# Routed experts: a selection made pair by pair, gates on the outcome, a scatter in two rounded terms, three chunks outside the ring

## The chip, the cores and the metric

The kernel runs on one core of a Trainium2 chip. The metric is the device time of one execution in microseconds (us). Before the change it is 2018.83 us, the median of 3 runs (2018.33 to 2025.63). PE is TensorE (matrix products), DVE VectorE, ACT ScalarE, POOL GpSimd, and SP the engine that issues most transfers.

## What is computed

A network of three blocks over 256 tokens of 1024 channels, all in float32: a first block of two layers (modulated norms, feed-forwards, a pooling mixer, latent attention), then a hybrid mixer, then the part that the change touches, a mixture of 32 experts in 4 groups, each token going to the best group and to 2 experts in it:

```python
def hier_moe(h, w_rg, b_rg, w_re, b_re, w_eg, w_eu, w_ed):     # h: 256 tokens x 1024
    lg = xt @ w_rg + b_rg;  grp = argmax(lg);  p_grp = softmax(lg)[grp]
    le = (xt @ w_re + b_re)[group grp]                          # 8 logits
    top_p, top_i = lax.top_k(jax.nn.softmax(le, axis=-1), 2)
    gate = top_p / jnp.sum(top_p, axis=-1, keepdims=True) * p_grp
    expert = grp * EXPERTS_PER_GROUP + top_i
    ...
    def expert_block(args):                                     # EXPERT_FF = 512
        xb, e = args
        return (jax.nn.silu(xb @ w_eg[e]) * (xb @ w_eu[e])) @ w_ed[e]
    y = yb[dest] * gate_s
    return jax.ops.segment_sum(y, tok_s, num_segments=n_tok)    # added to x
```

## The kernel before

All weights are packed on the host into one stream of chunks, 128 partitions x 3072 floats (1536 KB) each, in the order in which they are used. There are 304 of them. SP loads them into a ring of six slots (`ring`): chunk n is issued once the counter `chunk_used` shows that chunk n - 6 has been read (lines 212 to 216). The experts' stage uses the last 128 chunks, 8 for each of 16 pairs of experts. What is fixed by hand: each engine has its own program with its own order, and semaphores join them.

Before the stage come a norm (`pre_norm(7)`), in which ACT squares X and takes a root, and `router()`: PE computes the 36 logits and turns H into token-major HTOK, which ACT copies out of PSUM (line 1685); DVE makes the two choices of each token, their gates (block 24) and the position of each token in its expert's list (POS), and the longest list. If that is at most CAP = 64, `sparse()` runs, as with these inputs.

In `sparse()` DVE first builds SEL, for all 32 experts a matrix of 256 tokens x 64 places that holds 1 where the token has that place (line 1942, two operations of 2048 columns), and SELG, the same times the gate (line 1948). PE transposes SELG (line 1198) and ACT copies it out as SELGT (line 1694). For each pair p of experts PE then does:

- gather: XE = HTOK x SEL, 16 products into psG, which DVE copies out (line 1959)
- gate_up: 32 halves of 128 x 512 weights against XE, into the two banks of psS; ACT takes silu of the gate (line 1697), DVE multiplies with the other (line 1953)
- turn: four transposes of the hidden rows (line 1148), copied out by ACT as HT (line 1700)
- down: 16 halves against HT, into psG; DVE copies the outcome to YS (lines 1965 and 1967)
- scatter: YS x SELGT summed over all pairs in the four banks of psA, 8 products in float32

A half is a sixth of a chunk, so gate_up reads 5 1/3 chunks and down 2 2/3. The order within a step is gate_up(p), scatter(p - 1), turn(p), gather(p + 1), down(p). A float32 product shows as two records on PE, a product of the rounded type (`parts`, float32r) and a transpose as one. In the end DVE adds the four banks of psA to X (`add_acc`, line 2407), and SP writes X out in one transfer (line 219). Outside the stage all `mm` calls share line 370, so rows are told apart by their tiles.

Of the kernel before, what the change touches and what calls it, by code (L numbers as in the profile page):

```python
# [18 lines left out]
P = 128  # L19
# [6 lines left out]
RING = 6  # L26
EPS = 1e-6
# [18 lines left out]
          ("moe", E * FE)]  # L46
# [30 lines left out]
def build(nc, stream, cols_d, ident_d, x_d, masks_d, out_d):  # L77
    ctx = ExitStack()
    with ctx:
# [120 lines left out]
        def _(sp):  # L200
# [156 lines left out]
        SEL, SELG, SELGT = blk(4, 4), blk(8, 4), blk(12, 4)  # L357
        HTOK, XE, YS = tiles(16, 2, D), tiles(18, 1, P), blk(20)
# [8 lines left out]
        def _(pe):  # L367
# [735 lines left out]

            def sparse():

                c0 = BASE["moe"]  # L1110

                def gather(r, p):

                    if p == 0 and isinstance(r, int):
                        pe.wait_ge(sem("sp_sel"), 1)

                        pe.wait_ge(sem("sp_gt"), NP // 2)
                    for b in range(2):
                        for k in range(4 * b, 4 * b + 4):
                            for t in range(TT):  # L1120
                                off = t * E * CAP + p * P
                                src = SEL[:, off:off + P] if isinstance(r, int) else \
                                    SEL[:, bass.ds(r * (3 * P) + off, P)]
                                last = mm(psG[:, b, (k % 4) * P:(k % 4 + 1) * P], HTOK[:, t, k * P:(k + 1) * P],
                                          src, start=(k % 4 == 0 and t == 0), stop=(t == 1))
                        last.then_inc(sem("sp_ga"), 1)

                def gate_up(r, p):

                    pe.wait_ge(sem("sp_xe"), r * 6 + 2 * (p + 1))  # L1130
                    c = c0 + 8 * p
                    for u in range(2):
                        for k in range(KT):
                            for e in range(2):
                                g = (u * KT + k) * 2 + e
                                if g % 6 == 0:
                                    arrived(pe, c + g // 6, r * 24)
                                last = mm(psS[64 * e:64 * e + 64, u, :], XE[:, k, e * CAP:(e + 1) * CAP],
                                          half(c, g), start=(k == 0), stop=(k == KT - 1))
                                if g % 6 == 5:  # L1140
                                    last.then_inc(chunk_used, 1)
                    last.then_inc(sem("sp_gu"), 1)

                def turn(r, p):

                    pe.wait_ge(sem("sp_act"), r * 3 + (p + 1))
# [4 lines left out]
                def down(r, p):  # L1151

                    pe.wait_ge(sem("sp_htout"), r * 3 + (p + 1))
                    c = c0 + 8 * p
                    for h in range(2):
                        if p < NP - 1 or not isinstance(r, int):

                            pe.wait_ge(sem("sp_xe"), r * 6 + (2 * (p + 1) + h + 1))
                        for f in range(FE):
                            for e in range(2):  # L1160
                                g = 2 * 2 * KT + (h * FE + f) * 2 + e
                                if g % 6 == 0:
                                    arrived(pe, c + g // 6, r * 24)
                                last = mm(psG[64 * e:64 * e + 64, h, :], HT[:, f, e * CAP:(e + 1) * CAP],
                                          half(c, g), start=(f == 0), stop=(f == FE - 1))
                                if g % 6 == 5:
                                    last.then_inc(chunk_used, 1)
                        if h == 0:
                            last.then_inc(sem("sp_dn"), 1)

                def scatter(r, p, final=False):

                    pe.wait_ge(sem("sp_ys"), r * 6 + 2 * (p + 1))
                    for m in range(KT):
                        src = SELGT[:, p * S:(p + 1) * S] if isinstance(r, int) else \
                            SELGT[:, bass.ds(r * (3 * S) + p * S, S)]
                        last = mm(psA[:, m // 2, (m % 2) * S:(m % 2 + 1) * S], YS[:, m * P:(m + 1) * P], src,
                                  start=(isinstance(r, int) and p == 0 and m % 2 == 0), stop=final)
                    return last

                def step(r, p):
# [4 lines left out]
                    if not isinstance(r, int) or p < NP - 1:  # L1186
                        gather(r, p + 1)
                    down(r, p)


                pe.wait_ge(sem("sp_selg"), 1)
                pe.wait_ge(sem("htok_out"), 1)
                for p in range(NP):
                    b = p // 2
                    if p % 2 == 0 and b >= 2:
                        pe.wait_ge(sem("sp_gt"), b - 1)
                    for t in range(TT):
                        last = nc.tensor.transpose(psG[:, b % 2, ((p % 2) * 2 + t) * P:((p % 2) * 2 + t + 1) * P],  # L1198
                                                   SELG[:, t * E * CAP + p * P:t * E * CAP + (p + 1) * P], ident)
                    if p % 2 == 1:  # L1200
                        last.then_inc(sem("sp_gtps"), 1)
                gather(0, 0)
                step(0, 0)
                step(0, 1)

                with pe.Fori(0, 4) as r:
                    for j in range(3):
# [3 lines left out]
                scatter(0, NP - 1, final=True).then_inc(sem("moe_acc"), 1)  # L1211

            def dense():

                c0, t0 = BASE["moe"], 4 * NF
# [4 lines left out]
                for j in range(NP):  # L1220
                    if j >= 2:
                        pe.wait_ge(sem("dn_bc"), j - 1)
                    for i in range(2):
                        e = 2 * j + i
                        last = mm(psG[:, j % 2, i * S:(i + 1) * S], ident[0:E, e:e + 1].to_broadcast([E, P]),
                                  blk(25)[0:E, 0:S], start=(i == 0), stop=True)
# [4 lines left out]
                def step(r, p):  # L1231
                    c, n = c0 + 8 * p, t0 + 8 * p

                    for i in range(RING):
                        arrived(pe, c + i, r * 24)
                    for j in range(8):
                        e, f = divmod(j, FE)
                        pe.wait_ge(sem("act_ready"), r * 24 + (n + j - 1))
                        for u in range(2):
                            for k in range(KT):  # L1240
                                last = mm(psG[:, j % 2, u * S:(u + 1) * S],
                                          half(c, (u * KT + k) * 2 + e, f * P, P), H[:, k, :],
# [5 lines left out]
                    for h in range(2):  # L1248
                        for f in range(FE):
                            for e in range(2):  # L1250
                                g = 2 * 2 * KT + (h * FE + f) * 2 + e
                                if g % 6 == 0:
                                    arrived(pe, c + g // 6, r * 24)
                                for m in range(4 * h, 4 * h + 4):
                                    first = isinstance(r, int) and p == 0 and e == f == 0 and m % 2 == 0
                                    last = mm(psA[:, m // 2, (m % 2) * S:(m % 2 + 1) * S],
                                              half(c, g, (m % 4) * P, P), HD[:, e * FE + f, :],
                                              start=first, stop=(e == 1 and f == FE - 1))
                                if g % 6 == 5:
                                    last.then_inc(chunk_used, 1)  # L1260
# [6 lines left out]
                pe.sem_inc(sem("moe_acc"), 1)  # L1267
# [44 lines left out]
        def _(ac):  # L1312
# [378 lines left out]
            def sparse():  # L1691
                for b in range(NP // 2):
                    ac.wait_ge(sem("sp_gtps"), b + 1)
                    A(SELGT[:, b * 512:(b + 1) * 512], psG[:, b % 2, :], ACT.Copy).then_inc(sem("sp_gt"), 1)
                with ac.Fori(0, NP) as p:
                    ac.wait_ge(sem("sp_gu"), p + 1)
                    A(HSIL, psS[:, 0, :], ACT.Silu).then_inc(sem("sp_si"), 1)  # L1697

                    ac.wait_ge(sem("sp_ht"), p + 1)
                    A(HT.rearrange("p f s -> p (f s)"), psS[:, 0, :], ACT.Copy).then_inc(sem("sp_htout"), 1)  # L1700
# [32 lines left out]
            pre_norm(7)  # L1733
            router()
# [10 lines left out]
        def _(ve):  # L1745
# [191 lines left out]
            def sparse():  # L1937

                iot = iota[:, None, :].to_broadcast([P, E, CAP])
                for t in range(TT):  # L1940
                    sel = SEL[:, t * E * CAP:(t + 1) * E * CAP].rearrange("p (e s) -> p e s", s=CAP)
                    last = V.tensor_tensor(sel, iot, POS[:, t, :, None].to_broadcast([P, E, CAP]), ALU.is_equal)  # L1942
                link(last, "sp_sel")
                for t in range(TT):
                    sel = SEL[:, t * E * CAP:(t + 1) * E * CAP].rearrange("p (e s) -> p e s", s=CAP)
# [808 lines left out]
```

## Time and profile before

| | before |
|---|---|
| median of 3 runs | 2018.83 us |
| profiled execution | 2018.54 us |
| its span | 2016.7 us |
| PE busy / DVE / ACT | 91% / 49% / 33% |
| mean granted clock of PE | 0.945 |
| transfers, mean over the span | 240 GB/s, 304 chunks |

The span runs from the first to the last instruction of the profiled execution; the rest of its time lies around it. The granted clock is the share of full speed (2.4 GHz) that PE was given: 1.00 or 0.50 at a time, between them on average. Busy shares are averages over very different stages, so they do not say what bounds the last one.

### The profile page before, as it was taken

The numbers are of one execution on the slowest core, as the hardware profiler recorded it, in microseconds if no ns is written. First come the engines' busy times: TensorE is split into PE (matmuls) and PEld (weight loads), VectorE is DVE, ScalarE is ACT, GpSimd is POOL, SyncE is SP. The second block draws the span as 40 slices with busy tenths as digits, with TensorE's granted clock in tenths as the row PEclk, the third lists the DMA queues.
The fourth block names the chain that finished last, engine by engine and source line by source line (L and its number), as shares of the span: only waits on it lengthen the run. The fifth ranks groups of instructions, "written<-read, shape, count | busy, mean of one in ns | idle before, by whom it ended". The sixth has DMA issues, their size and how long they took to land.

```text
span 2016.7 us, 32388 instructions
## 1 busy us (share of the span) xinstructions
PE 1838.0 (91%) x13471; PEld 1516.9 (75%) x13471; DVE 988.3 (49%) x1398; ACT 665.3 (33%) x962; POOL 21.6 (1%) x14
## 2 busy tenths in 40 slices
PE   6999949999799988989998899988886999999998
PEld 3999938999799976779997799877873444434443
DVE  2977569886674545264455776456523111111111
ACT  3433324443434434354444533445411000000000
POOL 0000000000000000000000111000000000000000
PEclk8999968999899989989997999989987999999999
DMA  9988507887384421245441332422333999999996
GB/s 389 391 332 322 221 32 275 337 334 277 120 345 180 175 104 63 104 179 188 178 175 55 124 108 108 194 95 94 130 122 142 422 425 425 426 427 426 426 426 284
DMA packets 44589, 483.15 MB, mean 240 GB/s; under 512 B 4944, under 2 KB 5200, under 8 KB 5200
## 3 DMA queue, kind: packets, MB, share of 16 engines
q1 hardware_dynamic: 44352, 480.74, 60.4%
q8 instruction: 73, 1.20, 0.2%
q10 hardware_dynamic: 144, 1.05, 0.1%
q14 instruction: 20, 0.16, 0.0%
HBM read 480.72 MB, written 1.05 MB: 239 GB/s over the span
## 4 chain that ended last, share of the span: by engine, by line
PE 40%; DMA 8%; DVE 5%; ACT 2%; issue 1%; DVEq 0%; SPq 0%; ACTq 0%
PE psG L370 23%; PE psA L370 10%; DMA ring<-stream 8%; PE psS L370 5%; DVE parts L2099 1%; ACT parts L1482 0%; DVE mem L2114 0%; ACT mem L1649 0%; PE psS L1148 0%; DVE sg L2135 0%; PE psS L1022 0%; DVE mem L1948 0%; DVE mem L1942 0%; DVE mem L2381 0%; PE psG L1198 0%
## 5 line engine op out<-in xcount | busy, mean ns | idle before, releaser
L370 PE MATMUL psG<-parts 128*128 128x256 f32 x6016 | 787.2, 291 | 26.9 <-issue 9.0
L370 PEld LDWEIGHTS psG<-parts 128*128 128x128 f32 x6016 | 762.9, 199 | 37.9 <-issue 22.2
L370 PE MATMUL psA<-parts 128*128 128x256 f32 x2112 | 267.1, 283 | 0.0
L370 PEld LDWEIGHTS psA<-parts 128*128 128x128 f32 x2112 | 259.5, 192 | 0.0
L1774 DVE TENSOR_TENSOR parts<-ring,parts 128x2048 fp32r<-128x2048 f32 x84 | 192.2, 2288 | 115.1 <-ACT parts L1326 114.6
L370 PE MATMUL psS<-ring,mem 128*64 128x512 f32 (+1 forms) x1032 | 229.5, 594 | 12.7 <-DMA ring<-stream 11.0
L1326 ACT ACTIVATE parts<-ring 128x2048 fp32r<-128x2048 f32 x84 | 160.9, 1915 | 110.9 <-PE psA L370 110.9
L370 PEld LDWEIGHTS psS<-ring,mem 128*64 128x64 f32 (+1 forms) x1032 | 72.8, 137 | 164.9 <-issue 131.9
L1765 DVE SCALAR_TENSOR_TENSOR mem<-ring,silc,mem 128x1536 f32<-128x1536 f32 (+1 forms) x98 | 138.9, 1417 | 2.5
L2099 DVE TENSOR_TENSOR parts<-ring,parts 128x1024 fp32r<-128x1024 f32 x76 | 95.2, 1257 | 86.3 <-ACT parts L1482 85.2
L1697 ACT ACTIVATE mem<-psS 128x512 f32<-128x512 f32 x16 | 9.6, 597 | 367.9 <-PE psS L370 367.9
L1953 DVE TENSOR_TENSOR mem<-mem,psS 128x512 f32<-128x512 f32 x16 | 11.0, 688 | 233.6 <-ACT mem L1697 233.6
L1482 ACT ACTIVATE parts<-ring 128x1024 fp32r<-128x1024 f32 x76 | 79.8, 1054 | 138.4 <-PE psG L370 138.4
L370 PE MATMUL psA<-mem 128*128 128x128 f32 (+5 forms) x688 | 120.0, 335 | 4.0 <-DVE mem L2277 1.9
L1387 ACT ACTIVATE sg<-psG 128x256 f32<-128x256 f32 x88 | 33.8, 384 | 269.2 <-PE psG L370 269.2
L370 PEld LDWEIGHTS psA<-mem 128*128 128x128 f32 (+1 forms) x688 | 98.8, 192 | 28.7 <-issue 17.8
L370 PE MATMUL psG<-ring,mem 128*64 128x512 f32 x512 | 113.4, 595 | 0.7 <-ACT mem L1700 0.7
L1777 DVE TENSOR_TENSOR parts<-ring,parts 128x1024 fp32r<-128x1024 f32 x84 | 102.4, 1219 | 0.0
L1908 DVE TENSOR_TENSOR act<-sg,psG 128x256 f32<-128x256 f32 x88 | 37.1, 422 | 118.6 <-ACT sg L1387 115.3
L1327 ACT ACTIVATE parts<-ring 128x1024 fp32r<-128x1024 f32 x84 | 87.6, 1043 | 0.0
L370 PEld LDWEIGHTS psG<-ring,mem 128*64 128x64 f32 x512 | 35.3, 137 | 66.7 <-issue 64.0
L370 PE MATMUL psG<-mem 128*128 (+3 forms) x592 | 69.9, 287 | 3.6 <-ACT mem L1659 2.9
(335 smaller groups left out, 1418.8 us busy)
## 6 DMA issues: line engine op xcount, KB each, us to landing
ring<-stream SPq DMA_DIRECT2D x304, 1536.0 KB, 8.9
X<-x_in SPq DMA_DIRECT2D x1, 1024.0 KB, 17.5
mem<-masks ACTq DMA_DIRECT2D x1, 1024.0 KB, 4.7
x_out<-X SPq DMA_DIRECT2D x1, 1024.0 KB, 3.9
cst<-consts SPq DMA_DIRECT2D x1, 240.0 KB, 2.8
cols<-cols_in SPq DMA_DIRECT2D x1, 224.0 KB, 2.6
```

The source lines that it names most:

```text
L370: return nc.tensor.matmul(out, lhsT, rhs, start=start, stop=stop, skip_group_check=True)
L1326: A(WG[f % 2][:, 0, :], chunk(c, 0, 2 * SLOT), ACT.Copy).then_inc(sem("hi_gu"), 1)
L1327: A(WD[f % 3][:, 0, :], chunk(c, 2 * SLOT, CHUNK), ACT.Copy).then_inc(sem("hi_dn"), 1)
L1387: A(sg[:, t % 2, :], psG[:, t % 2, 0:S], ACT.Silu).then_inc(sem("silu_ready"), 1)
L1482: A(WS[s % 3][:, 0, :], chunk(c, a, a + SLOT), ACT.Copy).then_inc(sem("slot_hi"), 1)
L1697: A(HSIL, psS[:, 0, :], ACT.Silu).then_inc(sem("sp_si"), 1)
L1765: ins = V.scalar_tensor_tensor(out, w[:, q], silc[:, k:k + 1], out, ALU.mult, ALU.add)
L1774: V.tensor_tensor(WG[f % 2][:, 1, :], chunk(c, 0, 2 * SLOT), WG[f % 2][:, 0, :], ALU.subtract).then_inc(sem("lo_gu"), 1)
L1777: V.tensor_tensor(WD[f % 3][:, 1, :], chunk(c, 2 * SLOT, CHUNK), WD[f % 3][:, 0, :], ALU.subtract).then_inc(sem("lo_dn"), 1)
L1908: V.tensor_tensor(act[:, f % 2, :], sg[:, f % 2, :], psG[:, f % 2, S:2 * S], ALU.mult).then_inc(sem("hidden"), 1)
L1953: V.tensor_tensor(HACT, HSIL, psS[:, 1, :], ALU.mult).then_inc(sem("sp_act"), 1)
L2099: V.tensor_tensor(WS[s % 3][:, 1, :], chunk(c, a, a + SLOT), WS[s % 3][:, 0, :], ALU.subtract).then_inc(sem("slot_lo"), 1)
```

## The change

1. SEL is no longer built for all experts. DVE makes it for one pair at a time in two buffers, two pairs ahead (`selection`, two comparisons of 128 columns).
2. The gates leave the selection. PE transposes the pair's plain selection and picks the gates of its 128 places with two products of two columns (`select`), ACT copies both out (SELT, and GSL, one gate for each partition).
3. The outcome of down is multiplied by the gate when it is copied out, and written in two rounded terms: ACT writes the high one, DVE the remainder. Scatter has 16 products of the rounded type instead of 8 in float32.
4. Three chunks of pair 0 (its halves from 30 on) are not in the ring any more but in nine blocks of `mem`, loaded from ACT's queue between the norm and the router. The ring's stream has 301 chunks.
5. The last scatter signals each of the four banks when it is done; DVE adds bank by bank, and SP writes X out in four quarters.
6. PE's loop has 2 rounds of 6 steps instead of 4 of 3, those of ACT and DVE 6 rounds of 2 instead of one step a round. The dense branch, which does not run here, is adapted.

```diff
-          ("moe", E * FE)]
+          ("moe", E * FE - EARLY)]                                # EARLY = 3
...
-            sp.wait_ge(x_ready, 4 * 9)
-            sp.dma_start(out_d, X[:, :, :]).then_inc(sem("out_written"), 16)
-            sp.wait_ge(sem("out_written"), 16)
+            for b in range(4):
+                sp.wait_ge(x_ready, 4 * 8 + b + 1)
+                sp.dma_start(out_d[:, 2 * b:2 * b + 2, :], X[:, 2 * b:2 * b + 2, :]).then_inc(sem("out_written"), 16)
+            sp.wait_ge(sem("out_written"), 64)
...
+        SELT = part(5)[:, 0:512].rearrange("p (b s) -> p b s", b=2)
+        YS = part(6, 2).rearrange("p (h n) -> p h n", h=2)
+        EARLY_AT = (0, 1, 2, 3, 23, 25, 14, 15, 20)
...
+            def pair_half(r, p, g, a=0, n=512):
+                if p or not isinstance(r, int):
+                    return half(BASE["moe"] + 8 * p - EARLY, g, a, n)
+                if g < 48 - 6 * EARLY:
+                    return half(BASE["moe"], g, a, n)
+                a += (g % 2) * 512
+                return blk(EARLY_AT[(g - 48 + 6 * EARLY) // 2])[:, a:a + n]
...
+                def select(r, p):
+                    for t in range(TT):
+                        nc.tensor.transpose(psS[:, 1, t * P:(t + 1) * P], SEL[:, p % 2, t, :], ident)
+                    for t in range(TT):
+                        ...
+                        last = mm(psS[:, 1, S:S + 2], SEL[:, p % 2, t, :], gate, start=(t == 0), stop=(t == 1))
+                    last.then_inc(sem("sp_st"), 1)
...
                     for u in range(2):
+                        if u == 1:
+                            pe.wait_ge(sem("sp_stout"), r * 6 + (p + 1))
...
                     for m in range(KT):
-                        last = mm(psA[:, m // 2, (m % 2) * S:(m % 2 + 1) * S], YS[:, m * P:(m + 1) * P], src,
-                                  start=(isinstance(r, int) and p == 0 and m % 2 == 0), stop=final)
+                        for h in (1, 0):
+                            last = mm(psA[:, m // 2, (m % 2) * S:(m % 2 + 1) * S], YS[:, h, m * P:(m + 1) * P],
+                                      SELT[:, p % 2, :], ...)
+                        if final and m % 2 == 1:
+                            last.then_inc(sem("moe_acc"), 1)
...
+                def outcome(r, p, h):                              # ACT
+                    A(YS[:, 0, h * 512:(h + 1) * 512], psG[:, h, :], ACT.Copy, scale=GSL[:, p % 2:p % 2 + 1])
...
+            for i, b in enumerate(EARLY_AT):                       # ACT, after pre_norm(7)
+                nc.scalar.dma_start(blk(b), stream[NCHUNK + i // 3, :, (i % 3) * SLOT:(i % 3 + 1) * SLOT])
...
+                def selection(r, p):                               # DVE
+                    for t in range(TT):
+                        last = V.tensor_tensor(SEL[:, p % 2, t, :]..., iota..., pos..., ALU.is_equal)
+                def low(r, p):                                     # DVE
+                        V.scalar_tensor_tensor(YS[:, 1, ...], psG[:, h, :], GSL[:, p % 2:p % 2 + 1],
+                                               YS[:, 0, ...], ALU.mult, ALU.subtract)
...
-            ve.wait_ge(sem("moe_acc"), 1)
-            add_acc()
+            for b in range(4):
+                ve.wait_ge(sem("moe_acc"), b + 1)
+                V.tensor_tensor(X[:, 2 * b:2 * b + 2, :], ..., psA[:, b, :]..., ALU.add).then_inc(x_ready, 1)
```

PE at the start of the stage, from the router's last transpose on, before the change (psS<-ring,mem is gate_up, psG<-mem the gather):

```order
L1097 MATMUL psS<-cst,mem 1x128 [waits rt_max1]
L1303 TENSOR_LOAD most [waits rt_flag]
L1303 ISA x2
L1304 COMPARE_AND_BRANCH
L1198 MATMUL psG<-cst,mem 128x128 [waits htok_out,sp_selg]
L1198 MATMUL psG<-cst,mem 128x128 x7
L1198 MATMUL psG<-cst,mem 128x128 [waits sp_gt]
...
L370 MATMUL psG<-mem 128x128 [waits sp_gt,sp_sel]
L370 MATMUL psG<-mem 128x128 x15
L370 MATMUL psS<-ring,mem 64x512 [waits chunk_full2,sp_xe]
```

And now, to the end of the first pair's gate_up:

```order
L1322 COMPARE_AND_BRANCH
L376 MATMUL psG<-mem 128x128 [waits sp_sel,htok_out]
L376 MATMUL psG<-mem 128x128 x15
L1146 MATMUL psS<-cst,mem 128x128 x2
L376 MATMUL psS<-mem 128x2 x2
L376 MATMUL psS<-ring,mem 64x512 [waits chunk_full2,sp_xe]
...
L376 MATMUL psS<-ring,mem 64x512 [waits sp_stout]
...
L376 MATMUL psS<-ring,mem 64x512 [waits chunk_full0]
L376 MATMUL psS<-ring,mem 64x512 x5
L376 MATMUL psS<-mem 64x512 [waits early_in]
L376 MATMUL psS<-mem 64x512
```

The 32 transposes of line 1198 are gone and the gather stands right behind the branch; the last two halves of gate_up come from `mem`, not from the ring.

ACT before the change, from the norm's root to the first silu of the stage:

```order
L1330 ACTIVATE st<-psS,eps 128x64 [waits pre_sum]
L1685 ACTIVATE mem<-psA 128x2048 [waits rt_htok]
...
L1694 ACTIVATE mem<-psG 128x512 [waits sp_gtps] x8
L1695 UNCONDITIONAL_BRANCH
L1695 ISA
L1697 ACT_TABLE_LOAD
L1697 ACTIVATE mem<-psS 128x512 [waits sp_gu]
L1700 ACTIVATE mem<-psS 128x512 [waits sp_ht]
```

And now:

```order
L1348 ACTIVATE st<-psS,eps 128x64 [waits pre_sum]
L1783 DMA mem<-stream 128x1024 x9
L1703 ACTIVATE mem<-psA 128x2048 [waits rt_htok]
...
L1712 ACTIVATE parts<-psS 128x256 [waits sp_st]
L1715 ACTIVATE mem<-psS 64x1 x2
L1732 ACT_TABLE_LOAD
L1732 ACTIVATE mem<-psS 128x512 [waits sp_gu]
L1734 ACTIVATE mem<-psS 128x512 [waits sp_ht]
L1712 ACTIVATE parts<-psS 128x256 [waits sp_st]
L1715 ACTIVATE mem<-psS 64x1 x2
L1727 ACTIVATE parts<-psG,mem 128x512 [waits sp_dn,sp_stout]
L1727 ACTIVATE parts<-psG,mem 128x512 [waits sp_dn]
```

Nine transfers stand ahead of the HTOK copy, the eight copies of SELGT are gone, and each step has three small and two large copies more.

## Rows read from the trace of the kernel before

**Rows 1.** profile page, part 2: GB/s in each of the span's 40 slices

```profile
GB/s 389 391 332 322 221 32 275 337 334 277 120 345 180 175 104 63 104 179 188 178 175 55 124 108 108 194 95 94 130 122 142 422 425 425 426 427 426 426 426 284
```

**Rows 2.** chain that ended last, from 1500 us: start us, us, what

```profile
1520.91 4.50 DVE mem L1942 x2
1525.43 4.51 DVE mem L1948 x2
...
1529.98 2.93 PE psG L1198 x12
...
1536.86 3.82 PE psG L370 x32
...
1541.45 13.98 PE psS L370 x64
...
1568.07 13.73 PE psS L370 x64
...
1596.48 13.73 PE psS L370 x64
...
1682.92 13.54 DMA ring<-stream
```

**Rows 3.** stretches: us, busy of PE, PEld, DVE, ACT, POOL, then clock, DMA, GB/s

```profile
1497.00:1507.00 10.00, 9.24 (x42) 9.06 (x43) 4.01 (x46) 0.00 (x0) 0.00 (x0) 0.50 0.01 2
...
1530.00:1532.60 2.60, 2.60 (x12) 2.27 (x12) 0.00 (x0) 1.20 (x2) 0.00 (x0) 0.50 0.00 0
751.00:754.60 3.60, 3.47 (x8) 2.86 (x9) 3.47 (x8) 0.00 (x0) 0.00 (x0) 0.50 0.00 0
1499.00:1508.80 9.80, 9.23 (x44) 9.07 (x44) 5.38 (x54) 0.00 (x0) 0.00 (x0) 0.50 0.12 24
1600.00:1980.00 380.00, 369.94 (x1916) 177.85 (x1914) 44.92 (x65) 32.21 (x39) 0.00 (x0) 1.00 1.01 426
```

**Rows 4.** page, part 6: DMA issues, KB each, us to landing

```profile
ring<-stream SPq DMA_DIRECT2D x304, 1536.0 KB, 8.9
...
x_out<-X SPq DMA_DIRECT2D x1, 1024.0 KB, 3.9
cst<-consts SPq DMA_DIRECT2D x1, 240.0 KB, 2.8
```

**Rows 5.** DVE before the choice, grouped by shape: busy us, mean ns, idle before

```profile
L2438 DVE TENSOR_TENSOR mem<-mem 128x64 f32<-128x64 f32 x2 | 0.4, 224 | 0.1
```

**Rows 6.** instructions in time, ACT and its queue: start us, us, engine, line

```profile
1496.23 0.31 ACT L1330 ACTIVATE st<-psS,eps 128x64 f32<-128x64 f32 x1
1509.70 1.88 ACT L1685 ACTIVATE mem<-psA 128x2048 f32<-128x2048 f32 x1 [13.16 <-PE psA L1088]
...
736.87 0.39 ACTq L1724 DMA_DIRECT2D mem<-masks  x1
```

**Rows 7.** the same, PE, between the first pair's gate_up and down

```profile
1556.83 0.66 PE L1148 MATMUL psS<-cst,mem 128*128 128x128 f32 x4 [1.42 <-DVE mem L1953]
...
1560.99 7.09 PE L370 MATMUL psG<-ring,mem 128*64 128x512 f32 x32
```

**Rows 8.** the same, PE, first block's feed-forward

```profile
163.57 3.04 PE L370 MATMUL psA<-parts 128*128 128x256 f32 x24
...
175.09 1.40 PE L370 MATMUL psS<-cst,mem 128*128 128x1 f32 x12
```

**Rows 9.** the same, PE and DVE, the tail

```profile
1992.39 1.08 PE L370 MATMUL psS<-ring,mem 128*64 128x512 f32 x4 [0.90 <-DMA ring<-stream]
...
1998.25 7.09 PE L370 MATMUL psG<-ring,mem 128*64 128x512 f32 x32 [0.69 <-ACT mem L1700]
...
2005.38 0.69 DVE L1967 COPY mem<-psG 128x512 f32<-128x512 f32 x1 [2.74 <-PE psG L370]
...
2006.13 3.72 PE L370 MATMUL psA<-mem 128*128 128x256 f32 x16 [0.79 <-DVE mem L1967]
2009.88 2.48 DVE L2407 TENSOR_TENSOR X<-X,psA 128x512 f32<-128x512 f32 x4 [3.81 <-PE psA L370]
```

More of the change, by code:

```diff
@@ L26 @@
 RING = 6
+EARLY = 3
 EPS = 1e-6
@@ L1186, in step @@
                     if not isinstance(r, int) or p < NP - 1:
+                        select(r, p + 1)
                         gather(r, p + 1)
                     down(r, p)
-                pe.wait_ge(sem("sp_selg"), 1)
                 pe.wait_ge(sem("htok_out"), 1)
[L1193 to L1201, printed above, removed]
                 gather(0, 0)
+                select(0, 0)
                 step(0, 0)
                 step(0, 1)
-                with pe.Fori(0, 4) as r:
-                    for j in range(3):
+                with pe.Fori(0, 2) as r:
+                    for j in range(6):
                         step(r, 2 + j)
@@ L1937, in sparse @@
             def sparse():
[L1939 to L1945, printed above, removed]
-                    selg = SELG[:, t * E * CAP:(t + 1) * E * CAP].rearrange("p (e s) -> p e s", s=CAP)
-                    gate = blk(24)[:, t * E:(t + 1) * E][:, :, None].to_broadcast([P, E, CAP])
-                    last = V.tensor_tensor(selg, sel, gate, ALU.mult)
@@ L1949, in sparse @@
-                link(last, "sp_selg")
-                def hidden(p):
-                    ve.wait_ge(sem("sp_si"), p + 1)
+                def selection(r, p):
+                    if p >= 2 or not isinstance(r, int):
+                        ve.wait_ge(sem("sp_st"), r * 2 + (p - 1))
+                    for t in range(TT):
+                        a = t * E + 2 * p
+                        pos = blk(22)[:, 64 + a:66 + a] if isinstance(r, int) else blk(22)[:, bass.ds(r * 4 + (64 + a), 2)]
+                        last = V.tensor_tensor(SEL[:, p % 2, t, :].rearrange("p (e s) -> p e s", e=2),
+                                               iota[:, None, :].to_broadcast([P, 2, CAP]),
+                                               pos[:, :, None].to_broadcast([P, 2, CAP]), ALU.is_equal)
+                    last.then_inc(sem("sp_sel"), 1)
@@ L1974, in sparse, with step @@
-                hidden(NP - 1)
-                ys(NP - 1)
+                def low(r, p):
+                    for h in range(2):
+                        ve.wait_ge(sem("sp_yh"), r * 4 + (2 * p + h + 1))
+                        V.scalar_tensor_tensor(YS[:, 1, h * 512:(h + 1) * 512], psG[:, h, :], GSL[:, p % 2:p % 2 + 1],
+                                               YS[:, 0, h * 512:(h + 1) * 512], ALU.mult, ALU.subtract)\
+                            .then_inc(sem("sp_ys"), 1)
+                def step(r, p):
+                    hidden(r, p)
+                    if not isinstance(r, int) or p < NP - 1:
+                        xe(r, p + 1)
+                    if not isinstance(r, int) or p < NP - 2:
+                        selection(r, p + 2)
+                    low(r, p)
@@ L1977, in dense @@
+                selection(0, 0)
+                selection(0, 1)
+                xe(0, 0)
+                step(0, 0)
+                step(0, 1)
+                with ve.Fori(0, NP // 2 - 2) as r:
+                    for j in range(2):
+                        step(r, 2 + j)
+                step(0, NP - 2)
+                step(0, NP - 1)
             def dense():
                 ve.wait_ge(sem("dn_tr"), 1)
-                V.tensor_copy(blk(25)[0:E, 0:S], psS[0:E, 1, 0:S]).then_inc(sem("dn_gt"), 1)
+                V.tensor_copy(rstd[0:E, :], psS[0:E, 1, 0:S]).then_inc(sem("dn_gt"), 1)
```

142 lines of the change are left out of this document (85 added, 57 removed).

## The prediction

> **What bounds the kernel now.** I read the 40 slices first: from slice 32 on, about 1563 us, the transfers stand at 422 to 427 GB/s without a break [rows 1], while nearly all slices before it lie well below. That is the routed experts' stage. Then the chain of waits over that stretch: its pieces alternate between PE and "DMA ring<-stream", and in a middle pair 13.5 us of 29.5 are the transfer [rows 2]. Third, the stretches: from 1600 to 1980 PE is 97% busy at full granted clock, yet the transfers move 426 GB/s [rows 3]. A chunk is 1536 KB [rows 4], 1.573 MB, so 3.69 us at that rate, and a pair of experts takes 8 chunks, 29.5 us. PE alone needs 28.4 us for a pair: the second and third pair's gate_up start at 1568.07 and 1596.48 [rows 2], before the ring has been run down. So both limits are close, transfers are the slower one by 1.1 us a pair, and PE's busy share hides that.
>
> Three things follow. A faster PE inside the stage gives nothing. What counts is when the stream of refills starts, how many there are, and what is left after the last ones. Before: the first pair's gate_up starts at 1541.45 [rows 2]; a chunk is 6 of its 32 halves, 12 of 64 records in 13.7 us, so the first slot is free at 1544.05, and 122 refills follow. At 1992.39 PE gets the chunk it waits for last, the third from the end [rows 9]; the span ends at 2016.7, 24.3 us later.
>
> **Start of the stage.** Routing ends and DVE starts the selection tables at 1520.91. They take 4.50 us, their gated copies 4.51, then PE transposes with ACT copies until 1536.86, then the gather, 3.82 us, and gate_up at 1541.45 [rows 2]. All of the tables and transposes leave the path. In their place DVE makes the first pair's selection: two comparisons of 128 columns. 64 columns cost 0.22 us [rows 5] and 2048 cost 2.25 (half of 4.50), so by a line between them 0.29 each and 0.6 together, ends 0.45 and 4.5. PE gathers from 1521.55. The clock is late next: the warm-up that the transposes took on themselves now falls on the gather. The granted clock was 0.50 in the first 2.6 us after 1530 and in the first 3.6 after 751 [rows 3], the 1.2 GHz level. The warm gather has 32 records in 3.82, 0.12 each, so 0.24 at the low level: 11 in 2.6 us, 21 more in 2.5, 5.0 in all (ends 3.8 and 7.6). Gather ends at 1526.5, DVE copies for 0.69 [the size of the copy in rows 9] and gate_up starts at 1527.3, 14.15 us earlier. HTOK is ready: ACT's copy started at 1509.70 and took 1.88 [rows 6]. ACT's first copy of a selection has 8 us of gate_up to lie under.
>
> **The three early chunks.** Nine transfers of 512 KB leave ACT's queue after its last work of the norm, at 1496.5 [rows 6]. One issue took 0.39 us [rows 6], nine 3.5, and ACT is not wanted before 1509.70. They need 3 x 3.69 = 11.1 us of transfer, and between 1497 and 1507 there were 2 GB/s [rows 3]; what spills over delays the last filling of the ring by about 1 us, wanted 20 us later. So they cost nothing. What do they bring? 119 refills instead of 122 look like 11.1 us. But the ring keeps six slots. Gate_up of pair 0 frees five, the rest of pair 0 comes from the early blocks and frees none, and the next slot goes free only in pair 1. Pair 0 took 26.6 us (1541.45 to 1568.07 [rows 2]) and gets a select of 0.7 (below): pair 1 starts at 1554.6 and frees its first chunk at 1557.2, 27.3 us after the first release. Five refills take 18.5, so the stream stands still for 8.8. Of the 11.1 only 2.3 remain.
>
> From 1557.2 on 114 refills follow, 8 fewer than before followed 1544.05. Before, the time from the first release to the last wait was 1992.39 - 1544.05 = 448.3; less 8 x 3.69 = 29.5 that is 418.8. One stall grows: in that pair down starts 5.8 us after gate_up's end before (1555.2 to 1560.99 [rows 7]) and the five queued refills (18.5 us) end just as the next slot goes free (11.1 + 5.8 + 1.8 = 18.7). Now pair 1 stands there with scatter 1.9, turn 0.44, select 0.7 and gather 3.7 (1560.99 - 1556.83 - 0.44), 6.7 in all: 0.9 more. The last wait then ends at 1557.2 + 418.8 + 0.9 = 1976.9, 15.5 us earlier.
>
> **Work in each pair.** Scatter goes from 16 f32 records in 3.72 [rows 9] to 16 of the rounded type. The feed-forward's 24 such records took 3.04 [rows 8], so 2.03, 1.7 less. Select adds two transposes (four took 0.66, less than 0.3) and four records with a narrow right side (12 took 1.40 [rows 8], 0.45): 0.7, ends 0.3 and 1.0. A pair of PE alone becomes 28.4 - 1.7 + 0.7 = 27.4 against 29.5 of transfers: no gain and no loss, the cover is 2.1 us. The added waits (the orders of PE and ACT are shown with the change): gate_up's second half waits for ACT's copy of the selection, which is queued behind the copy of HT and starts during the gather, over 10 us early. Scatter waits for ACT's rounded copy and DVE's remainder, both under the next gate_up of 13.7 us. DVE's selection for two pairs on is behind its XE copies and needed a pair later.
>
> **The tail.** From the last wait: gate_up's last records 1.0, scatter 1.7 shorter, turn, copy, down. Down had ended at 2005.34 and ends 1.7 earlier. Then an ACT copy and a DVE remainder stand in a row where one DVE copy stood: DVE 0.75 as before, ACT 0.65 (down waited 0.69 for a copy of this size [rows 9]; ends 0.3, the 64-column row, and 1.88, the 2048-column row [rows 6]): 0.65 more. From scatter's start to the last add there were 6.2 us (2006.13 to 2009.88 + 2.48 [rows 9]); now the first bank can be added after four records, 0.6, and four adds of 0.62 follow: 3.1, so 3.1 less. The output went out as 1024 KB in 3.9; the last quarter is 256 KB, like the 240 KB that took 2.8 [rows 4]: 1.1 less, ends 0 and 1.3. Tail: 24.3 - 1.7 + 0.65 - 3.1 - 1.1 = 19.05.
>
> The fit in the Trainium skill (DMA: Bandwidth & Descriptors, Anatomy of one DMA) is a fixed 2.0 us plus bytes over 436 GB/s, taken on GpSimd's path. An estimate by it is 4.4 for the whole output and 2.6 for a quarter, 1.8 less; the trace has 3.9 for the whole, below the rule, and the sum keeps the row's 1.1, so by the rule the time would be 0.7 lower.
>
> **Sum.** Span 1976.9 + 19.05 = 1995.9, 20.8 less. The profiled execution took 2018.54, 1.84 over its span, and stands 0.3 under the median of 2018.83. Forecast: 2018.54 - 20.8 = 1997.7 us.
>
> **Rivals.** (a) The early chunks pay in full, 11.1 instead of about 1.4 net of both stalls: 1988. For it: the stage's transfers are the bound [rows 3], fewer bytes less time. Against: six slots cannot take a refill that has nowhere to go.
> (b) The clock does not rise with the gather and gate_up of pair 0 runs at the low level, 13.7 us longer: 2011.4. For it: from 1499 to 1508.8 PE was busy 9.23 of 9.8 us and the clock stayed at 0.50 [rows 3]. Against: that was the router's narrow work; dense 128-column work raised it after 2.6 us.
> (c) Slower. PE now waits some 2.1 us in each pair for chunks, instead of 1.1, and the clock falls in these waits. At the low level for w us a pair grows by w/2; it decides once w/2 is over the cover of 2.1, and the kernel is slower than before from 15 x (w/2 - 2.1) = 20.8 on, w = 7. At w = 10 the cost is 43.5: 2041. For it: after longer pauses around 1499 the clock was low [rows 3]. Against: from 1600 to 1980, with a wait in every pair, it was 1.00 throughout.
> The Trainium skill (TensorE: Matmul & The Clock Gate, HAM oscillation) describes this, a loop whose waits for data throttle PE again in every tile; the trace does not show it at waits of 0.9 us, and nothing here shows it at 2.
>
> **Chances.** Forecast with its errors 0.84, (a) 0.03, (b) 0.05, (c) 0.05, anything else 0.03. A measurement of this kernel tells about 0.5%, 10 us, from no change. Forecast and (a) lie beyond it, 0.87, and with the half of the rest that is mild 0.90 faster; (b) is within, 0.05; slower 0.05. The range: gather's ends -1.2 and +2.6, the output's -0.2 and +1.1, select and selection +1, rounding copy +1.2: 1994 to 2003; small errors in the stall and run to run widen it to 1993 to 2004, which leaves out (a), (b), (c) and little more.
>
> **What would show it.** Right: gate_up starting near 1527; refills idle for about 9 us between 1550 and 1560; the first pairs some 27.4 us apart and the later ones 29.5; the last wait near 1977 and 19 us behind it; 128x256 records of scatter at 0.12. Wrong: refills without a pause (a); a granted clock under 1 in pair 0 (b) or in later pairs (c); pairs clearly further apart than 29.5; ACT's table load or the issues on its queue late for HTOK.

## The result and the profile after

The changed kernel takes 2005.72 us (median of 4 runs, 2002.92 to 2006.30) against 2019.44 before: 13.7 us less; the ratio is 0.9926, interval 0.9910 to 0.9942. The forecast was 1997.7 with a range of 1993 to 2004: the sign is right, the size too large. The profiled execution took 2006.30, its span is 2004.5 where the sum had 1995.9. Five sections of the span show where the 8.6 us are:

| section, us | before | forecast | after | missed by |
|---|---|---|---|---|
| start of the span to the router's first product | 1499.73 | 1499.73 | 1500.47 | 0.7 |
| to gate_up of pair 0 | 41.72 | 27.6 | 29.57 | 2.0 |
| to the end of the last wait for a chunk | 450.94 | 449.6 | 453.57 | 4.0 |
| to the end of the last add | 19.97 | 15.8 | 16.23 | 0.4 |
| to the span's end | 4.34 | 3.2 | 4.66 | 1.4 |

The first section is not the change's: over the fourteen profiled kernels here it lies between 1497.68 and 1504.28 with all of that code the same but for nine issues on ACT's queue at its very end. That is a large part of the scatter of this kernel's times, and the reason why sections are compared here and not only totals.

The chain of waits of the changed kernel, start us, us, what. It answers to [rows 2]:

```profile
1522.22 0.51 DVE mem L1997 x2
...
1522.86 6.41 PE psG L376 x32
...
1530.04 13.98 PE psS L376 x64
...
1557.32 13.73 PE psS L376 x64
...
1584.85 13.73 PE psS L376 x64
...
1757.76 2.01 issue
1759.76 1.38 PE psS L376 x3
1761.14 3.96 issue
1765.11 16.19 PE psS L376 x61
...
1983.61 1.08 PE psS L376 x4
```

The two comparisons take 0.51 us together where 9 us of tables stood, and the transposes are gone. But the gather takes 6.41 instead of 3.82, and in the middle of the stage there is something that the kernel before does not have: PE stands 2.01 and 3.96 us, waiting for nothing that the profile shows, and the last 61 of gate_up's 64 records take 16.19. From the end of down at 1757.76 to scatter at 1781.30 it is 23.54 us, where a gate_up without a wait takes 13.73: 9.8 us more.

The stretches of the changed kernel (busy of PE, PEld, DVE, ACT, POOL, then clock, DMA share and GB/s), which answer to [rows 3]:

```profile
1522.90:1528.00 5.10, 5.10 (x24) 5.10 (x25) 0.91 (x3) 0.00 (x0) 0.00 (x0) 0.50 0.00 0
1550.00:1555.00 5.00, 5.00 (x25) 1.75 (x26) 1.38 (x4) 0.69 (x1) 0.00 (x0) 1.00 0.64 273
1555.00:1560.00 5.00, 5.00 (x26) 1.73 (x24) 1.22 (x2) 0.69 (x1) 0.00 (x0) 1.00 0.02 3
1757.00:1765.00 8.00, 2.14 (x7) 0.20 (x4) 0.75 (x1) 0.69 (x1) 0.00 (x0) 0.71 1.01 424
1765.00:1770.00 5.00, 4.89 (x12) 1.98 (x13) 0.00 (x0) 0.00 (x0) 0.00 (x0) 0.50 0.94 396
1770.00:1775.00 5.00, 5.00 (x24) 2.25 (x22) 0.00 (x0) 0.00 (x0) 0.00 (x0) 0.94 0.91 332
1775.00:1790.00 15.00, 15.00 (x97) 9.86 (x95) 2.47 (x5) 1.76 (x5) 0.00 (x0) 1.00 1.00 413
1790.00:1795.00 5.00, 5.00 (x26) 1.64 (x24) 0.75 (x1) 0.69 (x1) 0.00 (x0) 1.00 0.91 334
1795.00:1800.00 5.00, 5.00 (x26) 1.65 (x24) 0.75 (x1) 0.69 (x1) 0.00 (x0) 1.00 1.01 415
1600.00:1750.00 150.00, 144.06 (x813) 71.11 (x813) 20.56 (x36) 16.81 (x39) 0.00 (x0) 1.00 1.01 426
```

Four things are to be seen. The gather ran 5.1 us at the low level, not 2.6. The refills pause around 1557, as the prediction said. While PE stood at 1757 the transfers went on (424 GB/s) until the ring was full; then they ran short too (396 and less, up to 1800: against 426 GB/s 3.1 us of transfers are missing in these five stretches), and the clock was at its low level when PE came back. And from 1600 to 1750 PE is 96% busy and the clock never fell: PE's short waits in every pair did nothing to it.

The tail in order of time, to set beside [rows 9]:

```profile
1983.61 1.08 PE L376 MATMUL psS<-ring,mem 128*64 128x512 f32 x4 [1.24 <-DMA ring<-stream]
1984.62 2.18 PE L376 MATMUL psA<-parts 128*128 128x256 f32 x16
...
1987.92 7.09 PE L376 MATMUL psG<-ring,mem 128*64 128x512 f32 x32 [0.69 <-ACT mem L1734]
...
1995.06 0.69 ACT L1727 ACTIVATE parts<-psG,mem 128x512 fp32r<-128x512 f32 x1 [2.69 <-PE psG L376]
1995.78 0.75 DVE L2016 SCALAR_TENSOR_TENSOR parts<-psG,mem,parts 128x512 fp32r<-128x512 f32 x1 [2.62 <-ACT parts L1727]
1996.59 2.17 PE L376 MATMUL psA<-parts 128*128 128x256 f32 x16 [1.57 <-DVE parts L2016]
1997.36 2.48 DVE L2589 TENSOR_TENSOR X<-X,psA 128x512 f32<-128x512 f32 x4 [0.83 <-PE psA L376]
1998.08 2.13 SPq L221 DMA_DIRECT2D x_out<-X  x4
```

Scatter, rounding copy and staggered adds came out within 0.2 us of their prices. The last add ends at 1999.84, but the span goes on for 4.66 us. The page's line for the output shows a quarter at a median of 2.9 us to landing, where [rows 4] has 3.9 for the whole:

```profile
x_out<-X SPq DMA_DIRECT2D x4, 256.0 KB, 2.9
```

The median hides the last of the four: the longest landing in this trace is 4.3 us, which is the time from the end of the last issue (1998.08 + 2.13) to the span's end.

### The profile page after: what moved, and what is told of

Same layout as the page of the kernel before. It is cut to its first block, busy times and chain, and to the rows that moved or that the text cites. A ratio compares the mean times of both kernels' runs of the same rounds, so it can differ in the third digit from the quotient of the medians.

```text
span 2004.5 us, 32598 instructions
## 1 busy us (share of the span) xinstructions
PE 1826.9 (91%) x13535; PEld 1512.3 (75%) x13535; DVE 987.6 (49%) x1426; ACT 672.1 (34%) x1019; POOL 21.6 (1%) x14
## 3 DMA queue, kind: packets, MB, share of 16 engines
HBM read 480.72 MB, written 1.05 MB: 240 GB/s over the span
## 4 chain that ended last, share of the span: by engine, by line
PE 41%; DMA 6%; DVE 4%; ACT 2%; issue 1%; DVEq 0%; SPq 0%; ACTq 0%
PE psG L376 24%; PE psA L376 9%; PE psS L376 8%; DMA ring<-stream 6%; DVE parts L2161 1%; ACT parts L1500 0%; DVE mem L2176 0%; ACT mem L1667 0%; PE psS L1174 0%; DVE sg L2197 0%; PE psS L1028 0%; DVE mem L2443 0%; DVE mem L2420 0%; PE psA L1094 0%; DVE st L2426 0%
## 5 line engine op out<-in xcount | busy, mean ns | idle before, releaser
L376 PE MATMUL psA<-parts 128*128 128x256 f32 x2368 | 302.0, 284 | 1.6 <-DVE parts L2016 1.6
L376 PEld LDWEIGHTS psA<-parts 128*128 128x128 f32 x2368 | 291.0, 192 | 14.6 <-issue 12.2
L376 PE MATMUL psS<-ring,mem 128*64 128x512 f32 (+1 forms) x1028 | 233.5, 601 | 21.3 <-DMA ring<-stream 14.2
L376 PE MATMUL psG<-ring,mem 128*64 128x512 f32 x480 | 106.3, 596 | 0.7 <-ACT mem L1734 0.7
L376 PE MATMUL psG<-mem 128*128 128x128 f32 (+3 forms) x624 | 80.2, 310 | 5.1 <-ACT mem L1677 2.9
L376 PEld LDWEIGHTS psG<-mem 128*128 128x128 f32 (+2 forms) x624 | 67.9, 188 | 12.5 <-issue 6.5
L376 PE MATMUL psA<-mem,ring 128*128 128x256 f32 x240 | 56.5, 393 | 17.4 <-DVE mem L2079 13.6
```

The lines of the kernel that those rows point to most:

```text
L376: return nc.tensor.matmul(out, lhsT, rhs, start=start, stop=stop, skip_group_check=True)
```

## The experiments

Unless said otherwise a kernel differs from the changed one by its edit alone. "Middle" is the section from gate_up of pair 0 to the end of the last wait for a chunk, 450.94 us before and 453.57 after. Ratios are to the kernel before, which was measured anew beside each of three groups of kernels (2020.36, 2019.91 and 2019.77 us), so kernels of different groups are best compared by ratios and by sections.

**No loop on PE.**

```diff
-                with pe.Fori(0, 2) as r:
-                    for j in range(6):
-                        step(r, 2 + j)
-                for p in range(14, NP):
+                for p in range(2, NP):
                     step(0, p)
```

> The changed kernel with PE's steps of pairs 2 to 13 written out, no loop. Theory (the 5.97 us in which PE stood before and within the eighth pair's first products, with the low clock behind them, come from the jump back to the head of a loop of six steps): that stop is gone, the stream of refills does not pause there, and the time falls by 3 to 4 us to about 2002. Rival (PE stops wherever new code must be brought in): written out there is more new code, so there are several such stops and the time is the same or longer, 2005 to 2012.

2003.37 us, ratio 0.9914 (0.9901 to 0.9926). Its chain at the same pair:

```profile
1743.18 10.72 PE psG L376 x64
...
1754.06 14.40 DMA ring<-stream
```

The stop is gone, nothing took its place, and the middle is 451.06, 2.5 us shorter. New code alone does not stop PE; the stop comes with the jump back. The time was to be about 2002: it fell by less, and the interval of the ratio overlaps that of the changed kernel (0.9910 to 0.9942), so the stop is shown by the traces and its price by sections, not by the totals alone.

**The six-step loop in the kernel before.** The edit is the loop's form and the factors of its registers.

```diff
-                with pe.Fori(0, 4) as r:
-                    for j in range(3):
+                with pe.Fori(0, 2) as r:
+                    for j in range(6):
                         step(r, 2 + j)
```

> The kernel before with one edit: PE's experts loop as 2 rounds of 6 steps instead of 4 of 3. Theory (the stop belongs to the jump back in a loop of six steps): PE stops about 6 us when the second round begins, the clock falls, and the kernel is 3 to 6 us slower than before. Rival (the stop comes from something else in the changed kernel): no stop and the same time as before.

```profile
1759.85 10.59 PE psG L370 x64
1770.44 2.23 issue
1772.66 15.65 PE psS L370 x64
```

The stretches at the stop and behind it:

```profile
1770.00:1773.00 3.00, 0.78 (x6) 0.20 (x4) 0.69 (x1) 0.00 (x0) 0.00 (x0) 1.00 0.96 401
1773.00:1780.00 7.00, 7.00 (x28) 2.21 (x26) 0.00 (x0) 0.00 (x0) 0.00 (x0) 0.76 1.01 424
```

The stop appears in a kernel that had none, at the same jump, once and for 2.23 us, and the next gate_up takes 15.65 instead of 13.73, with the clock down after this stop of 2.2 us (0.76 in the seven us behind it). The middle grows from 450.94 to 454.30. Over all runs it is less: 2021.78 us, ratio 1.0011 (1.0000 to 1.0022). The expected size, 3 to 6 us, is missed; the stop itself is shown.

The traces also show what goes with it. The profile lists transfers of code in packets of 16 KB ("q8 instruction"). From 1700 to 1950 us, in which PE's loop of three steps jumps back twice, the kernel before has none of them: its body is not loaded again. With six steps there are 12:

```profile
q8 instruction: 12, 0.20, 0.3%
```

So here the body is loaded again as it runs. The packets come some 24 us apart, but at the jump one at 1765.1 and the next at 1769.8; PE stops at 1770.4. The changed kernel has one at 1756.9, just before its first stop (1757.8 to 1759.8), and one at 1762.6, inside its second (1761.1 to 1765.1). For that second stop:

```profile
q8 instruction: 1, 0.02, 1.7%
```

The kernel without the loop has none from 1751 to 1774. That PE waits for this code fits all of these; no run moved the code alone.

**The changed kernel again.**

> The changed kernel itself once more, on the same chip as these. Theory: 2004.5 to 2006.5; PE stops 6 to 7 us at the second round of its loop with the low clock behind it, the output's end comes 4 to 5 us after the last add. Rival (the stop was an accident of one execution): no stop, about 2003.

2007.23 us, ratio 0.9937 (0.9923 to 0.9951), 0.7 over the top of what was expected; PE stands 6.9 us in two pieces, the middle is 454.83, and the output ends 3.8 us after the last add, not 4 to 5. The stop is no accident: four profiles with this loop show 6.0 and 6.9 us (the changed kernel twice) and 6.6 and 6.8 (the next two kernels), and none of the kernels written out shows any.

**All chunks in the ring.**

```diff
-EARLY = 3
+EARLY = 0
```

> The changed kernel with no early chunks, all 128 in the ring. Theory (six slots decide: the early chunks let the refills pause for about 9 us in pair 0): only 1 to 2.5 us slower than the changed kernel, about 2007.5, and no pause of the refills in pair 0. Rival (the bytes taken out of the stream count in full): 11 us slower, 2016 to 2017.

2006.45 us, ratio 0.9930 (0.9915 to 0.9945), between the two measurements of the changed kernel. The middle is 455.31, 0.5 and 1.7 longer than theirs, but all three have the loop's stop in it, of a different length each (6.0, 6.9 and here 6.6 us). Up to that stop it can be read without it:

```profile
1758.88 2.23 issue
```

From gate_up of pair 0 that is 230.2 us, and 227.7 and 227.9 in the two profiles of the changed kernel: 2.4 us. Taking 4.7 MB out of the ring's stream in pair 0 was worth 1 to 2 us, not 11. Where the changed kernel had 3 GB/s, this one has:

```profile
1550.00:1555.00 5.00, 5.00 (x26) 1.61 (x24) 0.86 (x2) 0.69 (x1) 0.00 (x0) 1.00 0.93 354
1555.00:1560.00 5.00, 5.00 (x26) 1.70 (x24) 0.75 (x1) 0.69 (x1) 0.00 (x0) 1.00 1.01 425
```

**The early chunks held for pair 14.** The same nine transfers, with other contents.

```diff
+HELD = 14
...
-                if p or not isinstance(r, int):
-                    return half(BASE["moe"] + 8 * p - EARLY, g, a, n)
+                if p != HELD or not isinstance(r, int):
+                    return half(BASE["moe"] + 8 * p - shift(r, p), g, a, n)
```

> The changed kernel with the same nine early transfers at the same place, but holding the last three chunks of pair 14 instead of pair 0. Theory (the same bytes pay in full where the ring is short of chunks and not full): the refills do not pause in pair 0 and 3 x 3.69 us fewer remain at the end: 9 to 10 us faster than the changed kernel, 1995.5 to 1997. Rival (the early chunks bring what they bring, wherever they are used; the last wait moves with PE): no difference, 2005 to 2006.

2005.40 us, ratio 0.9918 (0.9905 to 0.9930). The time is the rival's; nothing like 9 us came. But from gate_up of pair 0 to the last add it takes 468.0 us, against 471.5 with all chunks in the ring and 469.8 and 471.1 in the changed kernel, so the place does matter a little. PE at the end of the stage:

```profile
1953.81 2.80 PE L377 MATMUL psS<-ring,mem 128*64 128x512 f32 x12 [0.65 <-DMA ring<-stream]
...
1971.10 13.90 PE L377 MATMUL psS<-ring,mem 128*64 128x512 f32 x64
```

The last wait is in pair 14, and pair 15 runs through without one: PE is the bound there. A chunk less saves 3.69 us of transfers, but PE is only 29.5 - 27.5 = 2.0 us a pair faster than the transfers, and just one pair was left in which to use it. So an early chunk pays under two conditions: its pair must not leave the ring full, and enough pairs must follow. That was tested next.

**One early chunk each in pairs 3, 5 and 7, and all three in pair 7.** Both on the version without PE's loop, with ACT's loop written out too.

```diff
+HELD = [(3, 7), (5, 7), (7, 7)]                   # pair, chunk of the pair
...
+        def ring_at(r, p, q):
+            before_it = EARLY if not isinstance(r, int) else sum(h < (p, q) for h in HELD)
+            return BASE["moe"] + 8 * p + q - before_it
```

> PE's steps written out as in u1_no_loop, and the three early chunks used one each as the last chunk of pairs 3, 5 and 7. Theory (an early chunk pays when a slot is never missing because of it; in one pair the ring can save at most what PE is faster than the transfers, so the chunks must lie in separate pairs, while about 2 us a pair are left for PE to catch up): from the first gate_up to the end 9 us less than u1_no_loop, 1994 to 1995.5. Rival (early chunks never pay more than they did in pair 0 or 14): the same as u1_no_loop, 2002 to 2004.

> As s1_spread_3_5_7, but all three chunks in pair 7. Theory: pair 7 frees only five slots, refills pause about 3 us, the rest pays: 5 to 6.5 us less than u1_no_loop, 1996.5 to 1998.5, and some 3 us more than the spread one. Rival (spreading does not matter in the middle of the stage): the same as the spread one.

Spread: 1994.44 us, ratio 0.9878 (0.9863 to 0.9892), middle 442.33, 8.7 less than without the loop alone. In pair 7: 1998.86 us, ratio 0.9892 (0.9878 to 0.9907), middle 443.76, 7.3 less. In pair 7 the middle gained more than the 5 to 6.5 us expected, and the time is 0.4 over the expected range. Its pause shows around 1765, between stretches of 424 and 430 GB/s, and is 1.8 us of transfers where 3 were expected:

```profile
1755.00:1760.00 5.00, 5.00 (x26) 1.72 (x24) 1.46 (x4) 0.69 (x1) 0.00 (x0) 1.00 1.01 424
1760.00:1765.00 5.00, 5.00 (x26) 1.72 (x24) 0.75 (x1) 0.69 (x1) 0.00 (x0) 1.00 0.83 351
1765.00:1770.00 5.00, 5.00 (x26) 1.59 (x23) 0.00 (x0) 0.00 (x0) 0.00 (x0) 1.00 0.88 344
1770.00:1775.00 5.00, 5.00 (x26) 1.58 (x22) 0.00 (x0) 0.00 (x0) 0.00 (x0) 1.00 1.01 430
```

The kernel without the loop has its early chunks in pair 0, so 7.3 and 8.7 us come on top of the 1 to 2 that they are worth there. The same bytes, loaded at the same time, are worth 1 to 2, 8 to 10 or 9 to 11 us by where they are used (an estimate: all chunks in the ring was only run with the loop, and writing out ACT's loop was not run alone). The spread version beats both kernels clearly. That spreading is better than pair 7 by 3 us was overrated: the middles differ by 1.4.

**One store.** On the version without the loop.

> As u1_no_loop, with the output written in one transfer after the last add, as in the kernel before. Theory (the last quarter of four waits for no less than one whole transfer took: 4.6 us from the last add's end to the span's end in the changed kernel, 4.3 before): the same within 0.5 us, or 0.3 faster. Rival (a quarter is quicker, as forecast): 1.1 us slower.

2005.77 us, ratio 0.9929 (0.9917 to 0.9941), against 2003.37 without this edit, intervals overlapping. From the last add to the span's end it took 5.71 us, with four stores 4.99; the kernels before had 4.34 and 4.27 with one store, and the others 3.66 to 5.35 with four. The time behind the last add scatters by more than the two forms differ (means 4.8 in three profiles with one store, 4.7 in eleven with four). A gain of 1.1 us is not seen; a smaller one, or a loss, stays open. The traces show one cost of the split: the same 1.05 MB go as 576 packets instead of 144. In 10 us around the output, in the kernel before (2007 to 2017) and in the changed one (1995 to 2005):

```profile
q1 hardware_dynamic: 144, 1.05, 25.4%
q1 hardware_dynamic: 576, 1.05, 31.8%
```

The packets keep the 16 transfer engines busy for 3.2 us where they took 2.5.

**Idle products to keep the clock up.** On the version without the loop, in the router: 28 of them, and then 58, each with 8 more just before the branch.

```diff
+                for _ in range(58):
+                    nc.tensor.transpose(psG[:, 0, 0:P], ident, ident)
                 pe.wait_ge(sem("rt_asg"), 1)
```

> As u1_no_loop, with 28 idle products of 128 columns on PE between HTOK's transposes and the counting of places, and 8 more before the branch; their results are not used. Theory (the first gather runs at the low granted clock for most of its 6 us): the clock is 1.00 when the gather starts, the gather takes 3.8 us, gate_up starts 2.2 us earlier after the router's start, 2001. Rival (the pause of over 2 us behind the branch lowers the clock again): the gather still takes 6 us and the time is that of u1_no_loop or more.

> As w1_warm, with 58 idle products instead of 28, so that PE is busy until the counting of places starts (in w1_warm it stood 3.9 us there and the clock fell again). Theory (the first gather costs 6 instead of 3.8 us for its low clock): the clock is 1.00 at the gather, the gather takes 3.8 us, and gate_up starts 1.5 to 2.2 us earlier after the router's start. Rival (the counting, its few narrow products and the pauses around them let the clock fall anyhow): gather 6 us, nothing gained.

2003.90 us, ratio 0.9919 (0.9906 to 0.9932), and 2003.68, ratio 0.9917 (0.9902 to 0.9932): nothing gained. The gather took 5.94 and 5.44 us (5.65 and 5.55 in the spread version and the one with pair 7, which have no idle products). The stretches of the longer one:

```profile
1520.00:1522.00 2.00, 1.94 (x19) 1.82 (x17) 1.69 (x10) 0.00 (x0) 0.00 (x0) 1.00 0.00 0
1522.00:1524.00 2.00, 0.77 (x8) 0.77 (x9) 1.59 (x8) 0.00 (x0) 0.00 (x0) 1.00 0.00 0
1524.00:1526.00 2.00, 0.62 (x6) 0.41 (x5) 0.94 (x5) 0.00 (x0) 0.00 (x0) 1.00 0.00 0
1526.00:1528.00 2.00, 2.00 (x12) 2.00 (x12) 0.02 (x1) 0.00 (x0) 0.00 (x0) 0.55 0.03 8
```

The clock was up until the gather began, and fell under the gather itself, behind 4 us in which PE was a third busy. The rival's outcome came. That these 2 us could be had by work inside the branch's pause was not tried.

**Spread chunks and idle products.**

> s1_spread_3_5_7 with the 58 and 8 idle products of w2_warm_long. Theory: both gains add, 1992.5 to 1993.5. Rival: as s1_spread_3_5_7, 1994.4.

1993.74 us, ratio 0.9869 (0.9852 to 0.9886); middle 442.30, gather 5.98. The intervals overlap and the sections agree: it is the spread version again.

**Scatter in float32.** On the version without the loop: ACT writes the gated outcome once, DVE's remainder is gone, 8 products instead of 16.

```diff
-                        for h in (1, 0):
-                            last = mm(psA[:, m // 2, (m % 2) * S:(m % 2 + 1) * S], YS[:, h, m * P:(m + 1) * P],
+                        last = mm(psA[:, m // 2, (m % 2) * S:(m % 2 + 1) * S], YS[:, 0, m * P:(m + 1) * P],
```

> As u1_no_loop, with scatter as 8 float32 products on an outcome that ACT writes once, gated, and without DVE's remainder. Theory (scatter's time in the pairs is hidden by transfers; only the last two scatters count): scatter 3.7 instead of 2.2 us, a pair of PE alone 29.1 against 29.5; the last wait is where it was, the tail is 1.5 longer for the last scatter but one, 0.8 shorter for the missing remainder, 1.1 longer to the last add: 1 to 2.5 us slower than u1_no_loop. Rival (the rounded scatter gains in every pair): 15 x 1.5 = 22 us slower.

2007.19 us, ratio 0.9935 (0.9920 to 0.9950), some 4 over the same kernel with the rounded scatter; 1 to 2.5 was expected, so the expectation was too small, but the rival's 22 is far off. The middle is 1.5 longer, from the last wait to the last add 1.9. Sixteen scatters became 1.55 us longer each, 25 in all, and 3.5 show.

```profile
1995.55 3.72 PE L376 MATMUL psA<-mem 128*128 128x256 f32 x16 [0.79 <-ACT mem L1722]
```

## Why the prediction was wrong

**What bounds the stage: right.** The refills are the bound; from 1600 to 1750 they move 426 GB/s, and pairs are 29.5 us apart. The float32 scatter shows that PE's work in the pairs is hidden: of the 22 us that fourteen longer scatters add in the middle, 1.5 came through.

**The step that failed first: "A pair of PE alone becomes 28.4 - 1.7 + 0.7 = 27.4 against 29.5 of transfers: no gain and no loss".** The pair is 27.53 us (1557.32 to 1584.85), but the change also made PE's loop one of six steps, and I priced its form at nothing: the prediction does not speak of it. In the trace PE stands 5.97 us when the second round begins, and its gate_up takes 3.8 us more than usual (1.38 and 16.19 for 13.73), most of it at the low clock. The cover of 2.0 us a pair cannot hide 9.8 us at one place, because the ring holds six chunks and no more: the refills run short there, by 3.1 us up to 1800. Without the loop the middle is 2.5 us shorter than in one profile of the changed kernel and 3.8 than in the other. The remaining 1.5 us of the missed 4.0 is in the middle of the loopless kernel as well (451.06 against 449.6). Most of it is bytes and not pauses: from the first release to the last wait 185.74 MB moved there and 189.89 before, 4.15 less where three chunks are 4.72, and the missing 0.57 MB are 1.3 us at 426 GB/s. Whose bytes they are was not followed. Even without the loop the kernel takes 2003.37 us, inside the range but 5.7 over the forecast, so the loop alone does not account for the miss.

**The early chunks: right, and the main lesson.** The forecast was a pause of 8.8 us and 1.4 us net. From the three stretches around 1557 (273, 3 and, from 1560 to 1565, 275 GB/s against 426) the pause is 8.5, and without the chunks the middle is 0.5 to 1.7 longer, 2.4 up to the loop's stop. Rival (a), 11.1 in full, was wrong for pair 0 and nearly right for chunks spread over pairs 3, 5 and 7.

**The start: right in kind, 2.0 us too short.** Gate_up came 12.15 us earlier after the router's start, for 14.15. 1.4 is the gather, 6.4 us for 5.0: I took the low clock for 2.6 us, the shorter of my two rows, and it lasted over 5. 0.6 is HTOK's transposes, which met the low clock for longer in this execution (3.65 us for 3.09); in the kernel without the loop they took 3.15. The clock was up before gate_up began (13.98 us, as before), so rival (b) did not happen.

**The tail: right but for the store.** From the last wait to the last add 16.23 for 15.8: the two copies are 1.57 us in a row where I had 1.40 and the adds begin 0.77 behind scatter's start for 0.6. The term "1.1 less" for the output was wrong: I took a transfer of 240 KB into the chip at an idle time for the last of four transfers out of it. Four stores of 256 KB go out within 2.1 us, in smaller packets, and the last landed after 4.3 us; how much of that is waiting behind the other three is not shown. An estimate by the fit in the Trainium skill (DMA: Bandwidth & Descriptors, Anatomy of one DMA), fixed 2.0 us plus bytes over 436 GB/s, is 2.6 for it and would have missed by more.

**Rival (c)** did not come from where I put it. Waits of up to 1.2 us for chunks, 14.2 us in all, left the clock at 1.00. But it was closer than I thought: in the kernel before with the six-step loop a stop of 2.2 us was enough to bring the clock down, and in the changed kernel it was down (0.54 from 1760 to 1765) right behind the first piece of the stop, 2.0 us.

## What to carry to other kernels

When a stream of transfers is the bound, count slots and not bytes: chunks taken out of a ring help only where the ring would otherwise be empty, one for each consumer step and early enough that the faster engine has steps left in which to use them. The same three chunks were worth 1 to 2 us in the first step, 7.3 us more than that together in the eighth, 8.7 more spread over the fourth, sixth and eighth. Price the form of a loop as well as its body, and look whether its code is loaded again on every round. Price a split store by its last piece.

## What the runs showed of the hardware

- A jump back to the head of PE's loop of six steps costs 2.2 to 6.9 us in which PE waits for nothing that the profile's waits show; with three steps the same jump costs nothing that can be seen, nor does straight code of all sixteen steps. Packets of code move at these stops, and none move while the three-step loop goes round (1700 to 1950 us); that PE waits for them is not shown by a run of its own.
- Waits for chunks of up to 1.24 us on PE left the granted clock at 1.00; behind stops of 2.0 and 2.2 us it was at the low level.
- The granted clock can fall after PE is busy again: it was 1.00 in a third-busy stretch of 4 us and fell under the dense work behind it.
- The same code before the stage took from 1497.7 to 1504.3 us over fourteen profiled executions; a change of 2 us here is only read from sections of the profile.
